# Recurrent gate products of a streaming encoder layer: plain fp32 against three products of rounded parts

## The reference, cut to what matters

```
r = sigmoid(xc @ w_rg + b_rg);  i = sigmoid(xc @ w_ig + b_ig)      # per head, 128x128 weights
log_a = -8 * r * softplus(-lambda);  a = exp(log_a)
u = sqrt(1 - a*a) * (i * xc);        h[t] = a[t] * h[t-1] + u[t]
y_lru = gelu(lru_gate) * h
```

## Time and profile before

| | before |
|---|---|
| runs, median | 1974.1 us |
| the profiled execution, whole | 1978.57 us |
| its span in the trace | 1977.0 us |
| TensorE busy (matmul) | 1918.2 us, 97% |
| VectorE busy | 1078.0 us, 55% |
| ScalarE busy | 725.0 us, 37% |
| GpSimd busy | 113.0 us, 6% |
| mean granted TensorE clock | 0.974 of full speed |
| G(0) to G(7) | 530.14 to 650.26 us |

### The profile page before, as it was taken

How to read it: one execution, slowest core, us unless ns; L and a number is a source line. 1 busy time by engine, 2 the same in 40 slices (tenths; PEclk the granted TensorE clock), 3 DMA queues, 4 the chain that set the end, 5 groups by cost and what they waited for, 6 DMA issues and landing times.

```text
span 1977.0 us, 31917 instructions
## 1 busy us (share of the span) xinstructions
PE 1918.2 (97%) x12877; PEld 1859.4 (94%) x12877; DVE 1078.0 (55%) x1355; ACT 725.0 (37%) x1141; POOL 113.0 (6%) x219
## 2 busy tenths in 40 slices
PE   8999999998899999999999999998799999999998
PEld 7999999998799999989998998987799999999998
DVE  6442443345687654566577677666745433442444
ACT  5221332223477644334545444542333221221222
POOL 2000000000012100001011010100000000000000
PEclk9999999999899999999998998997899999999999
DMA  4222222222222242334224323322622222222222
GB/s 140 74 70 75 68 83 73 76 67 84 91 72 74 72 119 86 95 98 124 78 70 113 103 78 111 96 69 78 224 76 65 74 75 76 74 76 76 75 66 77
DMA packets 268066, 171.68 MB, mean 87 GB/s; under 512 B 6534, under 2 KB 259642, under 8 KB 267677
## 3 DMA queue, kind: packets, MB, share of 16 engines
q1 hardware_dynamic: 239840, 129.52, 22.8%
q0 software_dynamic: 7072, 26.34, 4.3%
q10 hardware_dynamic: 21072, 14.69, 2.3%
HBM read 150.03 MB, written 20.48 MB: 86 GB/s over the span
## 4 chain that ended last, share of the span: by engine, by line
PE 85%; DVE 7%; ACT 3%; issue 2%; DMA 1%; DVEq 0%; ACTq 0%
PE pu L635 76%; PE pu L901 1%; DMA merged<-gate_spill 1%; PE pn L830 1%; PE pn L889 1%; ACT w_hi L977 1%; PE pn L858 1%; PE pn L840 1%; DVE h_t L1786 1%; PE pn L862 1%; DVE w_lo L1343 1%; DVE bc L1337 1%; DVE squares L1337 1%; PE pu L692 0%; DVE h_a L1793 0%
## 5 line engine op out<-in xcount | busy, mean ns | idle before, releaser
L1343 DVE TENSOR_TENSOR w_lo<-w_raw,w_hi 128x1024 fp32r<-128x1024 f32 x240 | 295.7, 1232 | 503.1 <-ACT w_hi L977 501.2
L635 PE MATMUL pu<-act_hi,w_hi 128*128 128x320 f32 x2336 | 542.3, 313 | 12.2 <-ACT act_hi L1004 7.4
L635 PE MATMUL pu<-act_lo,w_hi 128*128 128x320 f32 x2336 | 534.8, 310 | 2.1 <-DVE act_lo L1384 2.0
L635 PE MATMUL pu<-act_hi,w_lo 128*128 128x320 f32 x2336 | 534.0, 310 | 0.0
L977 ACT ACTIVATE w_hi<-w_raw 128x1024 fp32r<-128x1024 f32 x240 | 253.6, 1057 | 536.6 <-PE pu L635 532.9
L635 PEld LDWEIGHTS pu<-act_hi,w_hi 128*128 128x128 f32 x2336 | 394.4, 189 | 28.0 <-issue 21.0
L635 PEld LDWEIGHTS pu<-act_lo,w_hi 128*128 128x128 f32 x2336 | 391.9, 189 | 3.5 <-DVE act_lo L1384 3.1
L635 PEld LDWEIGHTS pu<-act_hi,w_lo 128*128 128x128 f32 x2336 | 392.8, 189 | 0.0
L635 PE MATMUL pu<-h_hi,w_hi 128*128 128x320 f32 x1056 | 241.7, 310 | 0.7 <-DVE ff_g L1401 0.7
L635 PE MATMUL pu<-h_lo,w_hi 128*128 128x320 f32 x1056 | 241.5, 310 | 0.0
L635 PE MATMUL pu<-h_hi,w_lo 128*128 128x320 f32 x1056 | 241.0, 309 | 0.0
(11 more groups left out here) (319 smaller groups left out, 1980.0 us busy)
## 6 DMA issues: line engine op xcount, KB each, us to landing
w_raw<-in_ffn_w_up_dram SPq DMA_DIRECT2D x87, 512.0 KB, 3.8
w_raw<-in_w_in_dram SPq DMA_DIRECT2D x73, 512.0 KB, 3.9
w_raw<-in_ffn_w_down_dram SPq DMA_DIRECT2D x32, 512.0 KB, 3.8
w_raw<-in_w_br_ssd_dram SPq DMA_DIRECT2D x16, 512.0 KB, 3.4
w_raw<-in_ffn_w_down_dram SPq DMA_DIRECT2D x16, 384.0 KB, 3.4
es<-e_spill POOLq DMA_DIRECT2D x40, 128.0 KB, 2.9
merged<-gate_spill POOLq DMA_DIRECT2D x8, 640.0 KB, 5.3
h_a<-in_state_ssd_h_dram POOLq DMA_DIRECT2D x8, 512.0 KB, 6.3
```

The source lines that it names most:

```text
L635: ins = pe.matmul(dst[:, h, :], w[:, side, c, :], a[:, k, h * HALF:(h + 1) * HALF], start=(at == 0), stop=(at == n - 1))
L1343: dve.tensor_tensor(w_lo[:, side, :, :], w_raw[:, side, :, :], w_hi[:, side, :, :].bitcast(F32), ALU.subtract).then_inc(s["w_lo_done"], 1)
```

## The change

`xc` and `w_gates` are now cut into rounded part and remainder as well. There are four new tiles and two new semaphores. ScalarE rounds, VectorE subtracts, and TensorE makes three fp32r products instead of one fp32 product, and waits for `gate_lo` alone, which both of VectorE's subtractions raise.

```diff
+            xc_hi, xc_lo = (sb(lru, n, [P, TOK], F32R) for n in ("xc_hi", "xc_lo"))
+            wg_hi, wg_lo = (sb(lru, n, [P, 2, P], F32R) for n in ("wg_hi", "wg_lo"))
...
             def lru_gates(j):
-                pe.wait_ge(s["wg_in"], j * 32 + 32)
-                pe.wait_ge(s["conv"], j * 2 + 3)
+                pe.wait_ge(s["gate_lo"], j * 2 + 2)
+                parts = ((wg_hi, xc_hi), (wg_lo, xc_hi), (wg_hi, xc_lo))
                 for w in range(2):
-                    for h in range(2):
-                        ins = pe.matmul(pn[w][:, h, 0:HALF], w_gates[:, w, :], xc[:, h * HALF:(h + 1) * HALF],
-                                        start=True, stop=True)
+                    for n, (wg, x) in enumerate(parts):
+                        for h in range(2):
+                            ins = pe.matmul(pn[w][:, h, 0:HALF], wg[:, w, :], x[:, h * HALF:(h + 1) * HALF],
+                                            start=(n == 0), stop=(n == 2))
                 ins.then_inc(s["gates_mm"], 1)
...   (ScalarE, lru_head)
+                act.wait_ge(s["wg_in"], j * 32 + 32)
+                act.activation(wg_hi[:, :, :], w_gates[:, :, :], ACT.Copy).then_inc(s["gate_hi"], 1)
+                act.wait_ge(s["conv"], j * 2 + 3)
+                act.activation(xc_hi[:, :], xc[:, :], ACT.Copy).then_inc(s["gate_hi"], 1)
                 take(U_LRU + 1, O_LRU + 1, 2, 2, j)
...   (VectorE, lru_head)
+                dve.wait_ge(s["gate_hi"], j * 2 + 1)
+                dve.tensor_tensor(wg_lo[:, :, :], w_gates[:, :, :], wg_hi[:, :, :].bitcast(F32), ALU.subtract).then_inc(s["gate_lo"], 1)
+                dve.wait_ge(s["gate_hi"], j * 2 + 2)
+                dve.tensor_tensor(xc_lo[:, :], xc[:, :], xc_hi[:, :].bitcast(F32), ALU.subtract).then_inc(s["gate_lo"], 1)
                 r = 1
                 take(U_LRU + r, O_LRU + r, 2, 2, j)
```

More of the change, by code:

```diff
@@ L142 @@
 sq_clear sq_done sq_part sq_added sq_summed ln_ready rs_act rs_step xn_done xh_done xl_done ff_th ff_s ff_hi ff_lo start_v start_a g1_in w_part0 w_part1 w_part2 w_part_hi w_part_lo g1_mm g1_cp hist_mm vec_mm
-hist_in ext_in conv tail_in wg_in gates_mm lru_v lru_a htail_in spill e_out es_in0 es_in1 yl_hi_done yl_lo_done
+hist_in ext_in conv tail_in wg_in gates_mm gate_hi gate_lo lru_v lru_a htail_in spill e_out es_in0 es_in1 yl_hi_done yl_lo_done
 dt_v dt_a dt_p gtr xb_th xb_out z_th m_built ht_zero ssd_p ssd_a ssd_v bseq
```

## The result

Four runs of the changed kernel took 1999.44, 2005.08, 2005.28 and 2006.94 us, median 2005.2 us, against 1974.9 us for four runs of before. The ratio is 1.0149, with a 95% interval of 1.0123 to 1.0175: the kernel is 1.5% slower. The forecast was 2005 us.

What follows compares the result with a forecast made beforehand. TensorE was taken as the bound, with a loop through ScalarE and VectorE almost as long. +23.5 us at full clock and +7.5 us for the clock make +31 us on 1974.1, 2005 us; range 1996 to 2013.

Steps and rivals of the forecast that it cites:

- The gates start behind xc_lo: At the gates, TensorE must wait until VectorE, after l_u, the scan and resid, has made xc_lo.
- Turns 0 and 1: G(0) starts 1.1 us late, G(1) at 553.6 instead of 546.38 behind the dt chain: +7.2 us in all.
- Turns 3 and 4 at full clock: G to G behind VectorE's queue: 19.54 us against 16.76 (+2.8) and 19.18 against 16.23 (+2.95).
- Turns 5 to 7 at full clock: G(4) to G(7) at 20.46 us a turn, 61.4 us against 50.20: +11.2 us.
- Turn 2: G(1) to G(2), with the small dt products: TensorE stays the bound, VectorE's path about 19.5 us; -0.35 us.
- The clock: TensorE's granted clock falls after each of six waits, slowing the gate products by 1.25 us each: +7.5 us.
- second rival: Clock low twice as long after each wait, over G and most of A: +41 us, 2015 us; chance 0.11.
- That it falls each time: At the gates, the low clock level was expected after each of the six waits of 3 us or more.
- The products themselves: Gate products on TensorE: twelve fp32r products take 1.80 us against 2.14 us for fp32, 0.35 us less per turn.
- Nothing is given back: Behind G(7) none of the loss returns; the rival that it does, 1974 to 1978 us, had chance 0.03.

Runs made afterwards that it cites:

- wait only: Kernel before, no cuts, old fp32 products, but TensorE's gates also wait for VectorE's resid of the turn before; 1992.5 us.
- early cuts: Changed kernel with the rounding and subtraction of the gate operands moved right behind l_u of the turn before, ahead of the scan and resid; 1978.8 us.
- filler run: Changed kernel with unread matmuls ahead of the wait for gate_lo, 20 in each of turns 3 to 7 and 40 in turn 1; 1996.5 us.
- delay runs: Kernel before with six, twelve or eighteen unread matmuls ahead of the gates of turn 1; 1974.2, 1973.9 and 1972.1 us.
- one product: Changed kernel with only the product of the two rounded parts in the gates, remainders still made and waited for; 2003.4 us.
- without subtractions: Changed kernel without VectorE's two subtractions; TensorE waits for ScalarE's roundings alone and makes the rounded parts' product three times; 1984.7 us.
- fp32 with waits: Changed kernel with the old fp32 gate products, all four parts still made and gate_lo still waited for; 2009.4 us.
- repeat with a delay: Changed kernel without VectorE's two subtractions, plus ten unread matmuls ahead of the gates of turn 2, on another chip; 1974.7 us, ratio 0.9998.

## Why the prediction was right, step by step

- **The gates start behind xc_lo.** Shown: wait only, early cuts and the waits in the trace. Turns 0 and 1: G(1) forecast at 553.6, measured 553.63, with 6.26 us of waiting ahead of it (about 6.5 forecast).
- **Turns 3 and 4 at full clock.** Forecast 19.54 and 19.18 us, in the filler run 19.51 and 19.17.
- **Turns 5 to 7 at full clock.** Forecast 61.4 us, in the filler run 60.0. The term was 1.4 us too large. I had taken all three turns from the one behind G(4), in which the last tap came 13.65 us behind the end of the gates (616.03 - 602.38); in the changed kernel it comes 13.3 us behind (653.75 - 640.46). The hand-over to TensorE is 0.05 us, where I took 0.10.
- **Turn 2.** Forecast 20.3 us, with TensorE as the bound and no wait. Here the step failed: TensorE waited 1.09 us, in the changed kernel and in the filler run (1.08) alike. I had kept what the low clock behind the dt products cost before (2.0 us by the delay runs: 20.69 against 18.69); in the filler run the clock was full, TensorE was ready earlier, and VectorE's path of 19.63 us (my estimate of it was 19.5) was the longer one. In the changed kernel the turn took 21.94 us, since the low stretch that turn 1's wait brought covered G(1) and lasted 6.8 us.
- **The clock.** Forecast +7.5 us for six waits. Measured were 8.9 us (127.2 - 118.3 from G(1) to G(7)) for the five ahead of G(1) and G(3) to G(6), where 5 x 1.25 = 6.25 were forecast, and G(7) itself ended another 0.9 us later. So the term was some 2 us too small, and the times from one G to the next show where. Behind G(3), G(4) and G(5) the clock was low for 3.4 us, and the next G came 1.2 to 1.5 us later than in the filler run, close to the 1.25 us forecast. Behind G(1) and G(6) it was low for 6.8 us, and the next G came 2.3 and 2.4 us later: that is the second rival (low for twice as long), to which I gave 0.11, and it held for two waits of six. Behind G(6), the second half of the 6.8 us:

```profile
661.20:664.60 3.40, 3.40 (x14) 3.40 (x14) 0.00 (x0) 2.48 (x3) 1.28 (x3) 0.50 0.57 168
```

- **That it falls each time.** There were six waits of 3.0 to 6.3 us in the changed kernel, and the granted clock fell at each of the six. The Trainium skill, "TensorE: Matmul & The Clock Gate", section "HAM oscillation — how this bites in real kernels", tells of a kernel that waits before every tile and has its clock lowered at every one; by that rule I had expected the fall each time, and this trace and the filler run agree. The runs beside it do not bear it out for every wait: with one product the clock stayed at 1.00 at a wait of 3.54 us, and in wait only at one of 2.64 us while it fell at another of 2.64. That all six waits of the profiled execution met it is in part luck.
- **The products themselves.** Forecast -0.35 us a turn. Where TensorE is the bound, in turns 3 and 4 without subtractions, a turn took 16.38 and 15.89 us against 16.76 and 16.23 before: 0.38 and 0.34 us less. fp32 with waits came out 4 us above the changed kernel. The Trainium skill, "FP8 and Floating Point Precision", section "TensorE Precision Notes", has a true fp32 product at four passes; if an fp32r product is one pass, which I assume, twelve passes replace sixteen. As an estimate that is a quarter less, 0.5 us of the 2.14 us; the trace has 0.34 to 0.38 us.
- **Nothing is given back.** The part behind the stage was 2.7 us shorter in the profile, within the 15 us by which it scatters.

G(4) to G(7) took 64.9 us, where about 65 was forecast with the clock, and the waits at the gates add up to 25.0 us for the 27 forecast (3.5 us each in turns 5 to 7 for 4.2, and 1.1 us in turn 2 for none). The total, 2005.2 for 2005, is nearer than the terms deserve: at full clock the sum was about 2 us too large and the clock's term about 2 us too small, and the part behind the stage moves by more than either. That the mechanism is right is shown; that the number came out within 0.2 us is luck.

What stays open is why the six runs without subtractions were all at 1981.7 to 1987.5 us, and the five with one product some 8 us above what their stage accounts for. The repeat with a delay shows for the first that it is not the work: nine of its twelve runs are at 1971.5 to 1976.3 us, and only three at 1981.6 to 1985.3, where all six had been. That a certain position against the clock's changes is a bad one for all executions of a kernel fits it, but the three delays of the kernel before did not show such a position.

## What to carry to other kernels

When a consumer is given a second operand to wait for, look up where its producer stands in that engine's queue, and read from the trace how late that place is; the producer's own length, here 0.83 us, says little. In a loop that runs through several engines, what is to feed the next turn has to be queued ahead of what finishes this one. And price a new wait of TensorE with the slower work behind it: here a wait of 3.0 to 3.5 us cost another 1.2 to 1.5 us where the clock was low for 3.4 us, 2.2 to 2.4 where it was low for 6.8, and nothing where it did not fall.

## What was not expected of the hardware

- The filler: 140 matmuls that do nothing made the kernel 9 us faster (2005.2 to 1996.5 us), because the granted clock stayed at 1.00 instead of a mean of 0.92 through the stage.
- Waits of the same length do not have the same effect on the clock. In the run with one product, waits of 3.08, 3.54 and 3.52 us at G(4) to G(6) were followed by 6.8, 0 and 3.4 us at the low level.
- The same instructions behind the stage took 1314.0 to 1329.8 us in the profiles of these kernels, with a mean granted clock between 0.965 and 0.982 in the runs. A difference of a few us between two such kernels is not told by a handful of runs of each; a reading of one stage in the trace tells it.
- A gain inside a stage that the trace shows plainly (9.5 us with one product) can be absent from the medians (1.8 us).
